# Attention's last product in a hybrid encoder block: values against turned probabilities, with the value tile rearranged

## The chip, the core and the metric

The kernel runs on one core of a Trainium2 chip. The metric is device time in microseconds (us), median of three runs. The engines are TensorE (PE), VectorE (DVE), ScalarE (ACT), GpSimd (POOL) and SyncE (SP), which only issues transfers here. Each has its own queue and works it off in order; they meet at semaphores.

## What is computed

One layer over 512 tokens of width 1024, in float32. Of the three branches between the two norms, the change touches attention: 8 heads of 64 columns, causal, with a forget bias.

```python
def forgetting_attention(q, k, v, f_logit, b_f):
    log_f = jax.nn.log_sigmoid((f_logit + b_f).astype(jnp.float32))
    F = jnp.cumsum(log_f, axis=1)
    ...
        logits = jnp.einsum('bqhd,bkhd->bhqk', q_i, k).astype(jnp.float32) * scale
        decay = F_q_i.transpose(0, 2, 1)[..., :, None] - F_k[..., None, :]
        mask = k_pos[None, :] <= pos_i[:, None]
        logits = jnp.where(mask, logits + decay, NEG_INF)
        p = jax.nn.softmax(logits, axis=-1)
        return jnp.einsum('bhqk,bkhd->bqhd', p.astype(v.dtype), v)
...
x = x + mixed @ w_out[l]
h = rms_norm(x, ffn_norm[l])
a, b = jnp.split(h @ w_gate_up[l], 2, axis=-1)
x = x + (jax.nn.silu(a) * b) @ w_down[l]
```

## The kernel before

**Numbers in two parts.** TensorE is fed tiles of type float32r. So that nothing of float32 is lost, each operand is kept as a high part (a copy in float32r) and a low part (the value less its high part). A product of two such operands takes three passes: high by high, high by low, low by high. For a weight tile of 128x1024, ACT writes the high part (`split_hi`, L741) and DVE the low one (`split_lo`, L1009). For an operand ACT runs `operand_hi` (L744) and DVE `operand_lo` (L1016).

**Units.** Weights come in units of 256 KB through three slots (`raw`, `whi`, `wlo`). `whole` (L450) is the product of a unit with all eight blocks of the activations: 24 matmuls of 512 columns, lines 436, 438 and 440.

**Stages.** norm, front, pair (four times, two heads each), mix (four times), out, the feed-forward stages. All loops are written out by hand on each engine, and the order of the work is the order of the code.

**A pair on TensorE** (L521 to L590): q and k (`whole` on units 0 and 1), five of eight blocks of v (unit 2), the logits of head 0 (L539, L541), two more blocks of v, the logits of head 1, the last block; conv's value column (unit 3), the turn of v by transposes (L549, bank 7), conv's gate (unit 4); the turn of head 0's probabilities (`turn_probs`, L561), six blocks of unit 5, the turn of head 1's, the last two blocks. Then comes what is changed: for each head, four blocks of tokens, three matmuls each (L584, L586, L588), of 512, 384, 256 and 256 columns. The stationary tile is the turned v of both heads, high (`V_HI`) or low (`V_LO`), 128 tokens by 128 value columns; the moving tile is a head's turned probabilities, high or low (`PT`). Head 0 goes to bank 7, head 1 to bank 3; half of the 128 rows of each result belong to the other head's columns, and are not used.

**What follows on ACT and DVE.** ACT writes the high part of a head's 64 rows from its bank (L862), DVE the low part (L1222), which frees the bank. DVE then runs the short convolution (L1230 to L1237, into `CY`), ACT and DVE split `CY`, then unit 8 of the stage's own count, that is unit 2 of the next pair. The next pair's q and k are worked out of banks 0 and 1 (ACT L820, L826, L831; DVE L1154, L1162). TensorE waits ahead of the next logits for banks 0 and 1 to be free and for `op_hi` (L528 to L530), which stands for L1154, L1162 and L831.

In mix, TensorE runs two gates (`whole`, twice) before `project` (L607) reads the attention output.

Of the kernel before, what the change touches and what calls it, by code (L numbers as in the profile page):

```python
# [19 lines left out]
ALU = mybir.AluOpType  # L20
# [38 lines left out]
    "op_hi": dict(norm=8, front=8, pair=15, mix=2, out=8, ffn_first=1, ffn=3),  # L59
    "op_lo": dict(front=4, pair=1, mix=2, ffn_first=1, ffn=3),  # L60

    "scalar_tile": dict(norm=12, front=2, out=8, ffn_first=3, ffn=3, down_a_end=4,
                        down_b_end=16),
    "vector_tile": dict(norm=8, front=2, pair=1, mix=2, ffn_first=3, ffn=3, down_b_end=16),
    "row_max": dict(pair=2), "exp_done": dict(pair=2), "probs": dict(pair=2),

    "vector_step": dict(norm=19, front=23, pair=15, mix=2, ffn_first=6, ffn=3, down_b_end=9),
# [12 lines left out]
def count(what, stage, i, k):  # L80

    before = 0
    for s, times, _ in STAGES:
        if s == stage:
            return before + i * RAISED[what].get(s, 0) + k
        before += times * RAISED[what].get(s, 0)
# [15 lines left out]
def hybrid_block(nc, x, attn_norm, w_in, b_forget, b_gate, w_proj_attn, pool_w, pool_scale,  # L102
# [26 lines left out]
    with ExitStack() as ctx:  # L129
# [3 lines left out]
        def sem(name):  # L133
            return ctx.enter_context(nc.semaphore(name))
# [30 lines left out]
        QS, KK = [T0, T0 + S], [T0 + 2 * S, T0 + 3 * S]  # L165
        K_LO, V_HI, V_LO = [T0 + S * j for j in (4, 5, 6)]

# [20 lines left out]
        def op(at, n=S, rows=slice(0, P)):  # L188
            return operands[rows, at:at + n]

        def half_rows(a):

            return slice(a * HD, (a + 1) * HD)

        def pt_at(j):

            return PT_AT[j] + (P if j == TB - 1 else 0)
# [7 lines left out]

        VT, CV, CB, CY = 0, 1, 2, 3
        GA, ACC, TMP = 0, 3, 4
# [41 lines left out]
        scalar_tile, vector_tile = sem("scalar_tile"), sem("vector_tile")  # L249
        row_max, exp_done, probs = sem("row_max"), sem("exp_done"), sem("probs")  # L250
        vector_step = sem("vector_step")
        consts = sem("consts")
# [11 lines left out]
        def wait_free(eng, b, stage, i, k):  # L264

            eng.wait_ge(free[b], count(f"free{b}", stage, i, k))
# [154 lines left out]
        def _(pe):  # L421
# [99 lines left out]
            with pe.Fori(0, WB) as i:  # L521
# [52 lines left out]
                for a, b, k in ((0, 7, 2), (1, 3, 5)):  # L574
                    wait_free(pe, 7, "pair", i, 1)
                    for j in range(TB):
                        wait_free(pe, 3 + j, "pair", i, 3 + a)
                    begin(b, "pair", i, k)
                    for j in range(TB):
                        first = min(j, TB - 2)  # L580
                        dst = banks[b][:, first * P:S]
                        n, at = S - first * P, PT_AT[j]
                        vj = slice(j * P, (j + 1) * P)
                        nc.tensor.matmul(dst, op(V_HI)[:, vj], op(PT[a][0] + at, n),  # L584
                                         start=(j == 0), stop=False)
                        nc.tensor.matmul(dst, op(V_HI)[:, vj], op(PT[a][1] + at, n),  # L586
                                         start=False, stop=False)
                        mm = nc.tensor.matmul(dst, op(V_LO)[:, vj], op(PT[a][0] + at, n),  # L588
                                              start=False, stop=(j == TB - 1))
                    mm.then_inc(full[b], 1)  # L590


            with pe.Fori(0, DB // 2) as i:
# [10 lines left out]
                whole(1, "mix", i, 1, 1, H_HI, H_LO)  # L604
                wait_free(pe, 7, "pair", 3, 2)
                wait_free(pe, 3, "pair", 3, 5)
                project(2, [(0, 3, 1), (1, 4, 1)])  # L607
                whole(2, "mix", i, 3, 1, H_HI, H_LO)
                pe.wait_ge(op_lo, count("op_lo", "pair", 3, 1))
                project(4, [(2, 5, 1), (2, 6, 1)])  # L610
# [123 lines left out]
        def _(act):  # L734
# [8 lines left out]
            def operand_hi(dst, src, scale=1.0):  # L743
                nc.scalar.activation(dst, src, ACT.Copy, scale=scale).then_inc(op_hi, 1)  # L744
# [71 lines left out]
            with act.Fori(0, WB) as i:  # L816
# [32 lines left out]
                wait_full(act, 7, "pair", i, 1)  # L849
                operand_hi(op(V_HI), banks[7][:])  # L850
                split_hi("pair", i, 6)
# [7 lines left out]
                for a, b, k in ((0, 7, 2), (1, 3, 5)):  # L859
                    rows = slice(a * HD, (a + 1) * HD)  # L860
                    wait_full(act, b, "pair", i, k)
                    operand_hi(operands[rows, bass.ds(BR[0][0] + i * S, S)], banks[b][rows, :])  # L862
                act.wait_ge(vector_tile, count("vector_tile", "pair", i, 1))
# [123 lines left out]
        def _(dve):  # L987
# [161 lines left out]
            with dve.Fori(0, WB) as i:  # L1149
# [54 lines left out]
                split_lo("pair", i, 5)  # L1204
                operand_lo("pair", i, 4, op(V_HI), op(V_LO), banks[7][:], None, 7)
                split_lo("pair", i, 6)
# [12 lines left out]
                wait_free(dve, 2, "pair", i, 2)  # L1219
                for a, b in ((0, 7), (1, 3)):  # L1220
                    rows = slice(a * HD, (a + 1) * HD)
                    operand_lo("pair", i, 13 + a, operands[rows, bass.ds(BR[0][0] + i * S, S)],  # L1222
                               operands[rows, bass.ds(BR[0][1] + i * S, S)], banks[b][rows, :],
                               None, b)

# [203 lines left out]
```

## Time and profile before

| | |
|---|---|
| Time, median of 3 runs | 845.84 us (845.74 to 847.63) |
| Span of the profiled execution | 846.0 us |
| TensorE busy | 828.2 us, 98% |
| TensorE weight loads (beside the matmuls) | 679.0 us, 80% |
| DVE busy | 433.0 us, 51% |
| ACT busy | 294.4 us, 35% |
| DMA, share of 16 engines | 32% |
| One pair | 45.0 us, four of them from about 58 to 235 us |

The span runs from the first to the last instruction of the one execution that was profiled, and lies 0.16 us above the median of the runs, so a difference in the span is read as one in the time. Busy time of matmuls overlaps: a matmul of 512 columns is shown as 0.39 us long, while the next starts 0.23 us after it.

### The profile page before, as it was taken

To read this page: it belongs to the slowest core of one execution; us is meant where nothing else is said; L and a number is where in the kernel's file an instruction comes from. 1 tells how busy PE (TensorE), PEld (TensorE's weight loads), DVE (VectorE), ACT (ScalarE), POOL (GpSimd) and SP (SyncE) were. 2 spreads that over 40 slices of the span, in tenths; PEclk is the share of its full clock that TensorE was granted. 3 is DMA by queue.
4 is the path that set the end of the run, shared out by engine and by line. 5 is a ranking of instruction groups with operands and counts; after the bars stand their busy time and mean duration, and the time that the engine had idled before them with its cause. 6 is when DMAs were issued, how large, how long until landed. Compare 5 with 4: busy or idle time off the path is not lost.

```text
span 846.0 us, 11118 instructions
## 1 busy us (share of the span) xinstructions
PE 828.2 (98%) x3691; PEld 679.0 (80%) x3691; DVE 433.0 (51%) x636; ACT 294.4 (35%) x466; POOL 3.6 (0%) x12
## 2 busy tenths in 40 slices
PE   5999999999999999999999999999999999999996
PEld 5777878787888888888888888888888888888884
DVE  6867585767753444344344555555555555323224
ACT  7355354443533222223323533222222222213113
POOL 1000000000000000000000000000000000000000
PEclk9989999999999999999999999999999999999998
DMA  6321222222223323333533223333333342222212
GB/s 212 100 76 50 76 74 74 74 74 75 74 75 100 99 76 98 101 97 99 173 125 100 76 75 99 99 99 99 99 99 99 99 119 101 102 97 89 94 46 100
DMA packets 126857, 80.27 MB, mean 95 GB/s; under 512 B 4796, under 2 KB 116980, under 8 KB 126836
## 3 DMA queue, kind: packets, MB, share of 16 engines
q1 hardware_dynamic: 126836, 80.00, 32.0%
q8 instruction: 12, 0.20, 0.1%
q14 instruction: 9, 0.07, 0.0%
HBM read 77.89 MB, written 2.10 MB: 95 GB/s over the span
## 4 chain that ended last, share of the span: by engine, by line
PE 95%; DVE 3%; ACT 1%; DMA 0%; issue 0%; SPq 0%; DVEq 0%; ACTq 0%
PE bank L436 23%; PE bank L440 23%; PE bank L438 23%; PE bank L628 6%; PE bank L626 6%; PE bank L630 6%; PE bank L541 1%; PE bank L539 1%; PE bank L561 1%; PE bank L467 1%; DVE operands L1018 1%; PE bank L586 1%; PE bank L584 1%; PE bank L588 1%; ACT work L747 0%; DMA big_x<-in_x_dram 0%
## 5 line engine op out<-in xcount | busy, mean ns | idle before, releaser
L436 PE MATMUL bank<-operands,whi 128*128 128x512 f32 x872 | 342.4, 393 | 0.9 <-DVE operands L1018 0.9
L438 PE MATMUL bank<-operands,whi 128*128 128x512 f32 x872 | 339.6, 390 | 0.0
L440 PE MATMUL bank<-operands,wlo 128*128 128x512 f32 x872 | 339.6, 389 | 0.0
L1009 DVE TENSOR_TENSOR wlo<-raw,whi 128x1024 fp32r<-128x1024 f32 x139 | 170.1, 1225 | 216.6 <-ACT whi L741 214.5
L436 PEld LDWEIGHTS bank<-operands,whi 128*128 128x128 f32 x872 | 163.9, 188 | 37.0 <-issue 3.3
L440 PEld LDWEIGHTS bank<-operands,wlo 128*128 128x128 f32 x872 | 163.8, 188 | 34.2
L438 PEld LDWEIGHTS bank<-operands,whi 128*128 128x128 f32 x872 | 163.9, 188 | 33.7 <-issue 0.2
L741 ACT CAST whi<-raw 128x1024 fp32r<-128x1024 f32 x139 | 145.0, 1043 | 130.1 <-PE bank L630 97.9
L626 PE MATMUL bank<-whi,operands 128*128 128x512 f32 x240 | 93.4, 389 | 0.0
L630 PE MATMUL bank<-whi,operands 128*128 128x512 f32 x240 | 93.4, 389 | 0.0
L628 PE MATMUL bank<-wlo,operands 128*128 128x512 f32 x240 | 93.4, 389 | 0.0
L744 ACT ACTIVATE operands<-work 128x512 f32 (+1 forms) x38 | 24.0, 632 | 166.1 <-DVE work L1337 112.9
L626 PEld LDWEIGHTS bank<-whi,operands 128*128 128x128 f32 x240 | 45.1, 188 | 9.4
L630 PEld LDWEIGHTS bank<-whi,operands 128*128 128x128 f32 x240 | 45.1, 188 | 9.4
L628 PEld LDWEIGHTS bank<-wlo,operands 128*128 128x128 f32 x240 | 45.1, 188 | 9.2
L1016 DVE TENSOR_TENSOR operands<-work,operands 128x512 f32 (+1 forms) x38 | 26.3, 692 | 36.0 <-ACT operands L744 36.0
L878 ACT ACTIVATE work<-bank,vecs 128x512 f32<-128x512 f32 x24 | 16.6, 690 | 79.2 <-PE bank L440 79.2
L1250 DVE TENSOR_TENSOR work<-bank,work 128x512 f32<-128x512 f32 x24 | 15.8, 688 | 41.2 <-PE bank L440 29.6
L1329 DVE TENSOR_TENSOR work<-bank,big_y 128x512 f32<-128x512 f32 x22 | 15.2, 691 | 36.7 <-PE bank L440 36.7
L747 ACT ACTIVATE work<-work 128x512 f32<-128x512 f32 (+1 forms) x24 | 15.2, 632 | 50.8 <-DVE work L1326 49.5
L1016 DVE TENSOR_TENSOR operands<-bank,operands 128x512 fp32r<-128x512 f32 (+4 forms) x44 | 21.7, 539 | 20.3 <-ACT operands L744 20.3
L840 ACT ACTIVATE big_y<-big_y,stat 128x128 f32<-128x128 f32 (+3 forms) x32 | 17.6, 552 | 31.0 <-DVE stat L1191 31.0
(124 smaller groups left out, 444.2 us busy)
## 6 DMA issues: line engine op xcount, KB each, us to landing
raw<-in_w_in_dram SPq DMA_DIRECT2D x106, 256.0 KB, 3.1
raw<-in_w_gate_up_dram SPq DMA_DIRECT2D x88, 256.0 KB, 3.1
raw<-in_w_down_dram SPq DMA_DIRECT2D x44, 256.0 KB, 3.0
raw<-in_w_out_dram SPq DMA_DIRECT2D x16, 256.0 KB, 3.1
big_x<-in_x_dram SPq DMA_DIRECT2D x4, 512.0 KB, 3.7
raw<-in_w_proj_attn_dram SPq DMA_DIRECT2D x8, 256.0 KB, 2.8
raw<-in_w_proj_pool_dram SPq DMA_DIRECT2D x8, 256.0 KB, 3.2
raw<-in_w_proj_conv_dram SPq DMA_DIRECT2D x8, 256.0 KB, 2.9
```

The source lines that it names most:

```text
L436: nc.tensor.matmul(banks[b][:, 0:width], whi[:, s, w], op(hi + k * S), start=a, stop=False)
L438: nc.tensor.matmul(banks[b][:, 0:width], whi[:, s, w], op(lo + k * S), start=False, stop=False)
L440: mm = nc.tensor.matmul(banks[b][:, 0:width], wlo[:, s, w], op(hi + k * S), start=False, stop=z)
L626: nc.tensor.matmul(banks[b][:], op(hi + at, P), whi[:, s, w], start=a, stop=False)
L628: nc.tensor.matmul(banks[b][:], op(hi + at, P), wlo[:, s, w], start=False, stop=False)
L630: mm = nc.tensor.matmul(banks[b][:], op(lo + at, P), whi[:, s, w], start=False, stop=z)
L741: nc.scalar.copy(whi[:, s, :], raw[:, s, :]).then_inc(w_hi, 1)
L744: nc.scalar.activation(dst, src, ACT.Copy, scale=scale).then_inc(op_hi, 1)
L840: e = nc.scalar.activation(lg, lg, ACT.Exp, bias=stat[:, 16 + at:17 + at], accum_out=stat[:, 24 + at:25 + at])
L878: nc.scalar.activation(wk(GA + br), banks[b][:], ACT.Sigmoid, bias=vecs[:, bass.ds(i * 2 + (V_GATE + br * DB + mm), 1)]).then_inc(free[b], 1)
L1009: nc.vector.tensor_tensor(wlo[:, s, :], raw[:, s, :], whi[:, s, :].bitcast(F32), ALU.subtract).then_inc(w_lo, 1)
L1016: ins = nc.vector.tensor_tensor(lo, src, hi.bitcast(F32), ALU.subtract)
```

## The change

The v tile is kept once for each head, `VV[a]`. For each block of 128 tokens it has 128 columns: 64 of the head's v in high part, and the same 64 in low part beside them. Head 0 has its high part in the left half, head 1 in the right. So the stationary tile has high and low at once, and two passes (against the high and the low part of the probabilities) leave two halves in the bank: rows of high v, and rows of low v. Their sum is the head's output (with the product of both low parts, which three passes left out).

On TensorE the third matmul of each block is gone. ACT writes the high part of v in two instructions (64 of every 128 columns each), DVE the low part in two. After the products ACT copies the half with low v to SBUF (`PV_LO`), DVE adds the other half from the bank and stores the sum in `PV`, which frees the bank; ACT and DVE take high and low part from `PV`. The low parts now count on `op_lo`, three a pair, and TensorE in mix waits for that count where it waited for banks 7 and 3.

```diff
@@ -57,12 +57,13 @@
     "op_hi": dict(norm=8, front=8, pair=15, mix=2, out=8, ffn_first=1, ffn=3),
-    "op_lo": dict(front=4, pair=1, mix=2, ffn_first=1, ffn=3),
+    "op_lo": dict(front=4, pair=3, mix=2, ffn_first=1, ffn=3),
     "scalar_tile": dict(norm=12, front=2, out=8, ffn_first=3, ffn=3, down_a_end=4,
                         down_b_end=16),
     "vector_tile": dict(norm=8, front=2, pair=1, mix=2, ffn_first=3, ffn=3, down_b_end=16),
     "row_max": dict(pair=2), "exp_done": dict(pair=2), "probs": dict(pair=2),
+    "v_lo_part": dict(pair=2),
     "vector_step": dict(norm=19, front=23, pair=15, mix=2, ffn_first=6, ffn=3, down_b_end=9),
 }
@@ -163,7 +164,11 @@
         QS, KK = [T0, T0 + S], [T0 + 2 * S, T0 + 3 * S]
-        K_LO, V_HI, V_LO = [T0 + S * j for j in (4, 5, 6)]
+        K_LO = T0 + 4 * S
+        VV = [T0 + 5 * S, T0 + 6 * S]
         PT_AT = [0, 4 * P, 7 * P, 9 * P]
@@ -192,6 +197,15 @@
             return slice(a * HD, (a + 1) * HD)
+        def v_part(a, low):
+            at = HD * (a if not low else 1 - a)
+            return op(VV[a]).rearrange("p (j c) -> p j c", c=P)[:, :, at:at + HD]
+        def v_turned(a):
+            return banks[7][:].rearrange("p (j c) -> p j c", c=P)[:, :, a * HD:(a + 1) * HD]
         def pt_at(j):
             return PT_AT[j] + (P if j == TB - 1 else 0)
@@ -203,7 +217,7 @@
         def wk(slot, n=S, rows=slice(0, P)):
             return work[rows, slot * S:slot * S + n]
-        VT, CV, CB, CY = 0, 1, 2, 3
+        VT, CV, CB, CY, PV_LO, PV = 0, 1, 2, 3, 4, 5
         GA, ACC, TMP = 0, 3, 4
         A1, SG, B1, HD_ = 0, 1, 2, 3
         JUNK_OUT, JUNK, FG = 5, 2, 4
@@ -248,6 +262,7 @@
         op_hi, op_lo = sem("op_hi"), sem("op_lo")
         scalar_tile, vector_tile = sem("scalar_tile"), sem("vector_tile")
         row_max, exp_done, probs = sem("row_max"), sem("exp_done"), sem("probs")
+        v_lo_part = sem("v_lo_part")
         vector_step = sem("vector_step")
         consts = sem("consts")
         pool_w_hi, pool_w_lo = sem("pool_w_hi"), sem("pool_w_lo")
@@ -581,11 +596,9 @@
                         dst = banks[b][:, first * P:S]
                         n, at = S - first * P, PT_AT[j]
                         vj = slice(j * P, (j + 1) * P)
-                        nc.tensor.matmul(dst, op(V_HI)[:, vj], op(PT[a][0] + at, n),
+                        nc.tensor.matmul(dst, op(VV[a])[:, vj], op(PT[a][0] + at, n),
                                          start=(j == 0), stop=False)
-                        nc.tensor.matmul(dst, op(V_HI)[:, vj], op(PT[a][1] + at, n),
-                                         start=False, stop=False)
-                        mm = nc.tensor.matmul(dst, op(V_LO)[:, vj], op(PT[a][0] + at, n),
+                        mm = nc.tensor.matmul(dst, op(VV[a])[:, vj], op(PT[a][1] + at, n),
                                               start=False, stop=(j == TB - 1))
                     mm.then_inc(full[b], 1)
@@ -602,11 +615,10 @@
                 whole(0, "mix", i, 0, 1, H_HI, H_LO)
                 whole(1, "mix", i, 1, 1, H_HI, H_LO)
-                wait_free(pe, 7, "pair", 3, 2)
-                wait_free(pe, 3, "pair", 3, 5)
+                pe.wait_ge(op_lo, count("op_lo", "pair", 3, 2))
                 project(2, [(0, 3, 1), (1, 4, 1)])
                 whole(2, "mix", i, 3, 1, H_HI, H_LO)
-                pe.wait_ge(op_lo, count("op_lo", "pair", 3, 1))
+                pe.wait_ge(op_lo, count("op_lo", "pair", 3, 3))
                 project(4, [(2, 5, 1), (2, 6, 1)])
                 whole(0, "mix", i, 5, 2, H_HI, H_LO)
                 whole(1, "mix", i, 6, 2, H_HI, H_LO)
@@ -847,7 +859,8 @@
                 wait_unit(act, "pair", i, 3)
                 nc.scalar.copy(wk(CV), banks[0][:]).then_inc(free[0], 1)
                 wait_full(act, 7, "pair", i, 1)
-                operand_hi(op(V_HI), banks[7][:])
+                nc.scalar.activation(v_part(0, False), v_turned(0), ACT.Copy)
+                operand_hi(v_part(1, False), v_turned(1))
                 split_hi("pair", i, 6)
                 wait_unit(act, "pair", i, 4)
                 nc.scalar.copy(wk(CB), banks[1][:]).then_inc(free[1], 1)
@@ -857,9 +870,13 @@
                         wait_full(act, 3 + j, "pair", i, 3 + a)
                         operand_hi(op(PT[a][0] + pt_at(j), S - j * P), banks[3 + j][:, j * P:S])
                 for a, b, k in ((0, 7, 2), (1, 3, 5)):
-                    rows = slice(a * HD, (a + 1) * HD)
                     wait_full(act, b, "pair", i, k)
-                    operand_hi(operands[rows, bass.ds(BR[0][0] + i * S, S)], banks[b][rows, :])
+                    nc.scalar.copy(wk(PV_LO, S, half_rows(a)), banks[b][half_rows(1 - a), :]
+                                   ).then_inc(v_lo_part, 1)
+                for a, b, k in ((0, 7, 2), (1, 3, 5)):
+                    rows = half_rows(a)
+                    wait_free(act, b, "pair", i, k)
+                    operand_hi(operands[rows, bass.ds(BR[0][0] + i * S, S)], wk(PV, S, rows))
                 act.wait_ge(vector_tile, count("vector_tile", "pair", i, 1))
                 operand_hi(opd(BR[2][0], i), wk(CY))
                 split_hi("pair", i, 8)
@@ -1202,7 +1219,11 @@
                                                       None, ALU.mult)
                     ins.then_inc(probs, 1)
                 split_lo("pair", i, 5)
-                operand_lo("pair", i, 4, op(V_HI), op(V_LO), banks[7][:], None, 7)
+                dve.wait_ge(op_hi, count("op_hi", "pair", i, 4))
+                for a in range(2):
+                    ins = nc.vector.tensor_tensor(v_part(a, True), v_turned(a),
+                                                  v_part(a, False).bitcast(F32), ALU.subtract)
+                ins.then_inc(free[7], 1)
                 split_lo("pair", i, 6)
                 split_lo("pair", i, 7)
                 for a in range(2):
@@ -1217,11 +1238,16 @@
                 nc.vector.tensor_tensor(wk(CV), banks[2][:], wk(CV), ALU.mult
                                         ).then_inc(free[2], 1)
                 wait_free(dve, 2, "pair", i, 2)
-                for a, b in ((0, 7), (1, 3)):
-                    rows = slice(a * HD, (a + 1) * HD)
+                for a, b, k in ((0, 7, 2), (1, 3, 5)):
+                    rows = half_rows(a)
+                    dve.wait_ge(v_lo_part, count("v_lo_part", "pair", i, a + 1))
+                    nc.vector.tensor_tensor(wk(PV, S, rows), banks[b][rows, :], wk(PV_LO, S, rows),
+                                            ALU.add).then_inc(free[b], 1)
+                for a, b, k in ((0, 7, 2), (1, 3, 5)):
+                    rows = half_rows(a)
+                    wait_free(dve, b, "pair", i, k)
                     operand_lo("pair", i, 13 + a, operands[rows, bass.ds(BR[0][0] + i * S, S)],
-                               operands[rows, bass.ds(BR[0][1] + i * S, S)], banks[b][rows, :],
-                               None, b)
+                               operands[rows, bass.ds(BR[0][1] + i * S, S)], wk(PV, S, rows))
                 def tap(k):
                     return vecs[:, bass.ds(i + (V_CONV + k * WB), 1)]
```

TensorE, head 0's product in a pair. Names: `operands` holds both v and the probabilities, and the bank is the output. Before:

```order
L584 MATMUL bank7<-operands 128x512 [waits free5,free6,free4,free7,free3]
L586 MATMUL bank7<-operands 128x512
L588 MATMUL bank7<-operands 128x512
L584 MATMUL bank7<-operands 128x384
L586 MATMUL bank7<-operands 128x384
L588 MATMUL bank7<-operands 128x384
```

And with the change:

```order
L599 MATMUL bank7<-operands 128x512 [waits free5,free6,free4,free7,free3]
L601 MATMUL bank7<-operands 128x512
L599 MATMUL bank7<-operands 128x384
L601 MATMUL bank7<-operands 128x384
L599 MATMUL bank7<-operands 128x256
```

One matmul of three is gone from each block, 8 in a pair and 32 in all; the waits ahead of the first are the same.

ACT, from the products of a pair to the high part of `CY` (`work`, the last row). Before:

```order
L744 ISA [waits full7]
L744 ACTIVATE operands<-bank7 64x512
L258 REGISTER_ALU
L744 ISA [waits full3]
L744 ACTIVATE operands<-bank3 64x512
L863 REGISTER_ALU
L744 ISA [waits vector_tile]
L744 ACTIVATE operands<-work 128x512
```

And with the change:

```order
L874 COPY work<-bank7 64x512 [waits full7]
L273 REGISTER_ALU
L874 COPY work<-bank3 64x512 [waits full3]
L756 ISA [waits free7]
L756 ACTIVATE operands<-work 64x512
L756 ISA [waits free3]
L756 ACTIVATE operands<-work 64x512
L880 REGISTER_ALU
L756 ISA [waits vector_tile]
L756 ACTIVATE operands<-work 128x512
```

Two copies stand ahead, and both high parts now come behind them and each behind a wait for DVE's sum.

DVE, from the convolution's first product (`bank2`) to its next step. Before:

```order
L1217 TENSOR_TENSOR work<-bank2,work 128x512 [waits free0]
L266 REGISTER_ALU
L1014 REGISTER_ALU [waits free2]
L1016 ISA [waits op_hi]
L1016 REGISTER_ALU
L1016 TENSOR_TENSOR operands<-bank7,operands 64x512
```

And with the change:

```order
L1238 TENSOR_TENSOR work<-bank2,work 128x512 [waits free0]
L281 REGISTER_ALU
L1244 TENSOR_TENSOR work<-bank7,work 64x512 [waits v_lo_part,free2]
L1244 TENSOR_TENSOR work<-bank3,work 64x512 [waits v_lo_part]
L1031 REGISTER_ALU [waits free7]
L1033 ISA [waits op_hi]
L1033 REGISTER_ALU
L1033 TENSOR_TENSOR operands<-work,operands 64x512
```

Two additions stand ahead of the low parts, each waiting for a copy of ACT.

## Rows read from the trace of the kernel before

**Rows 1.** The page: span, and busy time of each engine.

```profile
span 846.0 us, 11118 instructions
...
PE 828.2 (98%) x3691; PEld 679.0 (80%) x3691; DVE 433.0 (51%) x636; ACT 294.4 (35%) x466; POOL 3.6 (0%) x12
```

**Rows 2.** Waits of PE: waiter <- releaser, total us, times, longest; first and last.

```profile
PE bank L460 <- DMA bias_f<-in_b_forget_dram: 6.1, 1, 6.1
...
PE bank L485 <- DVE operands L1016: 0.8, 1, 0.8
```

**Rows 3.** Stretches: us, busy us (instructions) of each engine, granted clock, DMA share, GB/s.

```profile
60.00:105.00 45.00, 45.00 (x210) 35.90 (x209) 29.59 (x55) 19.53 (x42) 0.00 (x0) 1.00 0.26 69
...
195.00:240.00 45.00, 45.00 (x209) 35.91 (x208) 31.50 (x57) 20.76 (x44) 0.00 (x0) 1.00 0.25 70
```

**Rows 4.** Groups by line: busy us, mean ns of one, idle before; one of three alike.

```profile
L588 PE MATMUL bank<-operands 128*128 128x256 f32 (+2 forms) x32 | 10.3, 323 | 0.0
```

**Rows 5.** Timeline of PE, second pair: start, us, engine, line, operation.

```profile
140.90 0.39 PE L584 MATMUL bank<-operands 128*128 128x512 f32 x1
141.13 0.39 PE L586 MATMUL bank<-operands 128*128 128x512 f32 x1
...
142.82 0.40 PE L584 MATMUL bank<-operands 128*128 128x512 f32 x1
...
144.75 0.39 PE L436 MATMUL bank<-operands,whi 128*128 128x512 f32 x1
```

**Rows 6.** Timeline of DVE, same pair; in brackets the idle time before and its releaser.

```profile
139.70 1.69 DVE L1016 TENSOR_TENSOR operands<-bank,operands 128x512 fp32r<-128x512 f32 x4 [1.91 <-ACT operands L744]
...
143.99 0.68 DVE L1016 TENSOR_TENSOR operands<-bank,operands 64x512 f32 x1 [2.01 <-ACT operands L744]
145.83 0.69 DVE L1016 TENSOR_TENSOR operands<-bank,operands 64x512 f32 x1 [1.15 <-ACT operands L744]
...
151.29 1.23 DVE L1009 TENSOR_TENSOR wlo<-raw,whi 128x1024 fp32r<-128x1024 f32 x1
...
157.09 1.39 DVE L1162 TENSOR_TENSOR operands<-bank,operands 64x512 fp32r<-64x512 f32 x2 [1.90 <-ACT operands L826]
```

**Rows 7.** Timeline of ACT, same stretch.

```profile
143.14 0.59 ACT L744 ACTIVATE operands<-bank 64x512 f32 x1 [2.65 <-PE bank L588]
145.05 0.59 ACT L744 ACTIVATE operands<-bank 64x512 f32 x1 [1.32 <-PE bank L588]
149.69 0.63 ACT L744 ACTIVATE operands<-work 128x512 f32 x1 [4.04 <-DVE work L1237]
...
155.86 1.20 ACT L826 ACTIVATE operands<-bank 64x512 fp32r<-64x512 f32 x2 [2.30 <-PE bank L440]
157.09 1.25 ACT L831 CAST operands<-operands 64x512 fp32r<-64x512 f32 x2
```

**Rows 8.** Timeline of PE: the third pair's first matmul of logits.

```profile
159.06 0.28 PE L539 MATMUL bank<-operands 128*128 128x256 f32 x1
```

**Rows 9.** Groups by line and shape, 60 to 240 us: busy us, mean ns, idle before.

```profile
L1016 DVE TENSOR_TENSOR operands<-bank,operands 128x256 fp32r<-128x256 f32 x8 | 3.3, 416 | 0.0
...
L744 ACT ACTIVATE operands<-bank 128x256 fp32r<-128x256 f32 x8 | 3.1, 393 | 0.0
```

**Rows 10.** Timeline of ACT behind the high part of v, second pair.

```profile
133.40 0.59 ACT L853 COPY work<-bank 128x512 f32<-128x512 f32 x1 [3.21 <-PE bank L440]
```

**Rows 11.** Timeline of DVE behind the low part of v, second pair.

```profile
134.97 1.23 DVE L1009 TENSOR_TENSOR wlo<-raw,whi 128x1024 fp32r<-128x1024 f32 x1 [2.29 <-ACT whi L741]
```

**Rows 12.** Stretches in front (columns as in rows 3).

```profile
46.00:48.00 2.00, 2.00 (x11) 1.56 (x11) 1.87 (x2) 1.32 (x3) 0.00 (x0) 1.00 0.81 234
...
50.00:52.00 2.00, 2.00 (x5) 1.14 (x5) 1.76 (x2) 0.00 (x0) 0.00 (x0) 0.50 0.00 0
...
54.00:56.00 2.00, 2.00 (x8) 1.58 (x7) 0.72 (x1) 2.00 (x5) 0.00 (x0) 0.71 0.57 163
```

## The prediction

> **What bounds the kernel now.** I read the page's line of busy times first: TensorE is busy for 828.2 of 846.0 us, DVE and ACT for half and a third [rows 1]. Then the waits of TensorE: four entries, from 6.1 us down to 0.8, all of them at the start or in front [rows 2]. None lies in the pairs, where the change is: there TensorE is busy for all of every stretch of 45.00 us, at a granted clock of 1.00 (2.4 GHz), and DMA has a share of a quarter [rows 3]. So time that TensorE is spared in a pair is time of the kernel, as long as nothing new makes it wait, and a transfer, an ACT or a DVE instruction costs nothing as long as it is done when TensorE comes to need it. The rest is two questions: how much TensorE is spared, and whether the longer way from the products to the low parts stays under cover.
>
> **What TensorE is spared.** The group of L588 shows 32 matmuls and 10.3 us busy, and the groups of L584 and L586 the same [rows 4]. That is not the gain: matmuls overlap (the row at 140.90 is 0.39 us long, the next starts at 141.13), so it is starts that count. Head 0's twelve matmuls run from 140.90 to 142.82, which is 1.92 us; head 1's from there to the next block's first matmul at 144.75, 1.93 us [rows 5]. In each block the three passes have the same number of columns and the third goes, so a third of 3.85 us goes: 1.28 us a pair, and four times that is **5.13 us**. The bounds on this term: nothing if the places stay empty (a rival, below), and 10.3 us by the busy time, which would need matmuls that don't overlap; I take the starts, since they are what the same matmuls do in the same place. The moving columns, the number of weight loads for a matmul and the waits ahead of the first one are unchanged.
>
> The Trainium skill ("TensorE: Matmul & The Clock Gate", Back-to-back issue gap) gives a matmul N columns divided by 2.4 GHz plus 2.5 ns. For 512, 384, 256 and 256 columns that is 216, 163, 109 and 109 ns, 0.60 us a head, and an estimate by that page is 4.8 us for eight heads. The rows show 0.23 us where it has 0.216, and they decide.
>
> **What is added to the split of v.** ACT writes the high part in two instructions of 256 elements, at 0.39 us each by the nearest row, instead of one of 512 at 0.59; DVE the low part in two at 0.42 [rows 9] instead of one of 0.69. The new ones have runs of 64 columns, which no row has; dearest they would cost what one of 512 does, 0.6 and 0.7 us each. Some 0.15 us more on each engine, at worst 0.7. Behind it ACT next idles for 3.21 us until TensorE is done [rows 10], DVE for 2.29 us [rows 11], and the products start only at 140.90, some 9 us later. Nothing comes through: 0.
>
> **Head 1 comes sooner.** Its products wait for the low parts of its probabilities, which DVE ends at 139.70 + 1.69 = 141.39 [rows 6]. Head 1 now starts at 142.82 - 0.64 = 142.18 instead of 142.82 [rows 5]. So 0.79 us of slack are left of 1.43: 0. That DVE work idles for 1.91 us ahead [rows 6] and hangs on TensorE's transposes alone, so the split of v can't push it.
>
> **The new way from the products to the low parts.** I replay the second pair. Before, ACT starts on head 0 at 143.14, 0.32 us after the end of its products, and on head 1 at 145.05, 0.30 us after [rows 5, 7]. Ends are now 142.18 and 144.75 - 1.28 = 143.47, so ACT starts the copies at 142.50 and 143.77; each takes 0.59 us (an ACT instruction of 64x512 from a bank, [rows 7]; both bounds of it are near, a copy or cast of this size from anywhere shows 0.59 to 0.63). From ACT's end to DVE's start rows show 0.26 us (143.73 to 143.99) and 0.19 (145.64 to 145.83) [rows 6, 7]; I take 0.26. DVE adds at 143.35 to 144.04 and, behind the second copy (144.36), at 144.62 to 145.31, by 0.69 us a piece: a DVE instruction with a bank and SBUF as inputs on 64 rows [rows 6]. ACT writes the high parts from SBUF at about 144.4 to 145.0, and, 0.13 us behind the second sum, at 145.44 to 146.07, by 0.63 us [rows 7]. DVE writes the low parts at 145.35 to 146.04 and at 146.33 to **147.02**. Before, the last low part ended at 145.83 + 0.69 = 146.52 [rows 6]. So DVE's tail (the convolution, `CY`, unit 8, the low parts of q and k) is **0.5 us later** by the clock on the wall, while TensorE is 1.28 us earlier: together 1.8 us of slack are used in each step from pair to pair.
>
> What stood behind, and still fits: unit 8's low part ends at 151.29 + 1.23 = 152.52 [rows 6], now 153.02. TensorE needs it 48 matmuls behind the products. From 144.75 to 159.06 it has 63 matmuls [rows 5, 8], 0.227 us each, so 48 are 10.90 us and the need is at 155.65, now 154.37: 1.35 us are left. Then k. ACT's L826 starts at 155.86 when TensorE is done with k, after an idle 2.30 us [rows 7]; it now would start at 154.58 with 0.5 us of idle left. DVE's L1162 starts at 157.09 after an idle 1.90 us [rows 6], now at 155.81 with 1.90 - 0.50 - 1.28 = 0.12 us left. It ends 1.39 us later at 158.48 (ACT's L831 at 158.34), and the logits begin at 159.06 [rows 6 to 8]: 0.58 us. So 0.12 + 0.58 = **0.70 us** of cover remain ahead of the logits, three times in the kernel. Behind the fourth pair stand two gates, 48 matmuls again, before the attention output is read at about 10.9 us; the low parts are there 3.5 us behind the products' end, and the gates don't need them. Sum of all waits: 0.
>
> **Sum.** 845.84 - 5.13 = **840.7 us**, and a span of about 840.9.
>
> **Rivals.**
>
> *TensorE waits at the logits (part of the gain).* DVE's tail is the only place with little cover. Were each of the four hand-overs between ACT and DVE 0.26 us longer than I put it (twice the dearest on a row), the tail would be 1.04 us later, 0.34 beyond the cover; three steps give 1.0 us, and the time is 841.7. At 0.9 us beyond the cover in each step it is 843.4, which is about no gain. For it: the order of waits crosses between the engines twice now where it crossed once. Against: all pieces have near rows.
>
> *Nothing is gained.* The same wait at 1.3 to 1.7 us beyond the cover (a tail 2 us or more longer than the replay) would put the pairs at ACT's and DVE's pace, and only the fourth keeps its 1.28 us: 844.6 us, within the bound. That asks for added instructions at twice the rows' durations. That the compiler keeps the third matmul is excluded by the order of instructions: 8 fewer in a pair.
>
> *The clock falls (slower).* In front, TensorE is busy throughout, yet the granted clock goes from 1.00 (11 matmuls in 2 us) to 0.50 (5 in 2 us, 1.2 GHz), and is back in the stretch from 54 to 56 us [rows 12]. What runs ahead of the fall are 16 matmuls with 8 rows. A fall as long as that one, from about 48.5 to 55 us, costs about half of 6.5 us, 3.2 us. A pair has thin matmuls too, with 64 rows (L541), and a third of the full ones at its end now goes. Were that to bring one such fall into every pair, the time would be 840.7 + 12.8 = 853.5; from two falls in all, it is slower than before. Against it: the clock is 1.00 in all four pairs [rows 3], and 16 full matmuls and 48 more still follow there with no gap. The Trainium skill (same page, Part 1) has the throttle released by how busy the engine has been; by that rule there is no fall here, as no idle time is added, but the rows show a fall with the engine busy for the whole stretch, so the rule alone does not exclude it.
>
> **How the numbers follow.** Forecast, no wait: 0.82. Part of the gain: 0.07. Nothing gained: 0.05. Clock: 0.03. Another loss that I don't see: 0.03. A measurement of this kernel can tell about 0.3%, 2.5 us, from no change, so the bound is 843.3. Faster: 0.82 and most of the 0.07, 0.88. Same: the rest of it and the nothing, 0.07. Slower: 0.05. The range goes from 839.5 (the term 1.2 us larger, a quarter, or a faster median) up to 843.3: the median of before may stand up to 1.8 us under a single run, and the partial case is taken in.
>
> **What would show it.** TensorE's instructions fall by 32 in 3691, its busy time by up to 10.3 us, but the span by 5.1. The products take 2.57 us a pair (16 starts) and a pair 43.7 instead of 45.0. The list of TensorE's waits has no new entry; an entry at L539's place behind the low part of k, or an issue wait there, is the first rival. DVE's idle time ahead of the low part of k shrinks from 1.90 to about 0.1 us, ACT's ahead of k from 2.30 to 0.5. The first addition starts about 1.2 us behind head 0's last matmul start. The granted clock stays 1.00 from 60 us on. I am wrong if the pair's period falls by less than 1.2 us, if head 1's products start later than 1.3 us behind head 0's, or if a later stage gives the 5 us back.

## The result, and the profile after

| | before | after |
|---|---|---|
| First measurement, median | 845.79 us (845.65 to 847.63, 4 runs) | 839.74 us (839.62 to 840.14, 4 runs) |
| Ratio, first measurement | | 0.9923, 95% interval 0.9910 to 0.9935 |
| Ratio, more runs of the same two kernels | | 0.9942, 95% interval 0.9927 to 0.9957 |
| Span of the profiled execution | 846.0 us | 838.0 us |
| One pair, logits to logits | 45.02 us | 43.75 us |

The change makes the kernel faster. The forecast was 840.7 us, a ratio of 0.9939. The first measurement gave more: by its ratio the time is 845.84 * 0.9923 = 839.3 us, just below the low end of 839.5 (its median, 839.74 us, lies 0.2 us above that end). The second, with 23 runs of before and 6 of after, gave 0.9942.

The page of after, against [rows 1]:

```profile
span 838.0 us, 11082 instructions
...
PE 820.6 (98%) x3659; PEld 672.4 (80%) x3659; DVE 438.7 (52%) x648; ACT 299.2 (36%) x478; POOL 3.6 (0%) x12
```

TensorE has 32 matmuls fewer, DVE and ACT 12 instructions more each and 5.7 and 4.8 us more work. TensorE's waits answer to [rows 2]: four entries again (first and last shown), at the start and in front, none in the pairs, and the granted clock is 1.00 in all four pairs.

```profile
PE bank L475 <- DMA bias_f<-in_b_forget_dram: 6.5, 1, 6.5
...
PE bank L500 <- DVE operands L1033: 0.8, 1, 0.8
```

TensorE's timeline of the second pair's products, against [rows 5], and the third pair's logits, against [rows 8] (start, us, engine, line, operation):

```profile
137.28 0.39 PE L599 MATMUL bank<-operands 128*128 128x512 f32 x1
...
138.56 0.40 PE L599 MATMUL bank<-operands 128*128 128x512 f32 x1
...
154.16 0.28 PE L554 MATMUL bank<-operands 128*128 128x256 f32 x1
```

A head takes 1.28 us instead of 1.92. ACT and DVE behind it, against [rows 6] and [rows 7] (in brackets the idle time before, and what ended it):

```profile
138.76 0.58 ACT L874 COPY work<-bank 64x512 f32<-64x512 f32 x1 [1.89 <-PE bank L601]
140.06 0.58 ACT L874 COPY work<-bank 64x512 f32<-64x512 f32 x1 [0.71 <-PE bank L601]
...
141.49 0.63 ACT L756 ACTIVATE operands<-work 64x512 f32 x1 [0.20 <-DVE work L1244]
...
150.96 1.20 ACT L838 ACTIVATE operands<-bank 64x512 fp32r<-64x512 f32 x2 [1.05 <-PE bank L455]
```

```profile
139.44 0.68 DVE L1244 TENSOR_TENSOR work<-bank,work 64x512 f32<-64x512 f32 x1 [1.09 <-ACT work L874]
140.67 0.69 DVE L1244 TENSOR_TENSOR work<-bank,work 64x512 f32<-64x512 f32 x1 [0.54 <-ACT work L874]
141.55 1.44 DVE L1033 TENSOR_TENSOR operands<-work,operands 64x512 f32 x2 [0.19 <-issue]
...
152.19 1.39 DVE L1179 TENSOR_TENSOR operands<-bank,operands 64x512 fp32r<-64x512 f32 x2 [0.51 <-ACT operands L838]
```

The order is the one of the replay. The low parts end at 142.99, 5.71 us behind the products' start, where before they ended 5.62 behind it (146.52 - 140.90): the longer way delays them by 0.1 us, not 0.5.

But 8.0 us of span is more than four pairs give, which is 4 * 1.27 = 5.1 us. The first pair's logits start at 69.01 before and at 66.66 after: **2.35 us of the 8.0 lie ahead of all that was changed.** This the experiments had to explain.

### The profile page after: what moved, and what is told of

The parts are those of the page before. It is cut to its first block, busy times and chain, and to the rows that moved or that the text cites. A ratio compares the mean times of both kernels' runs of the same rounds, so it can differ in the third digit from the quotient of the medians.

```text
span 838.0 us, 11082 instructions
## 1 busy us (share of the span) xinstructions
PE 820.6 (98%) x3659; PEld 672.4 (80%) x3659; DVE 438.7 (52%) x648; ACT 299.2 (36%) x478; POOL 3.6 (0%) x12
## 4 chain that ended last, share of the span: by engine, by line
PE 94%; DVE 3%; ACT 1%; DMA 1%; SPq 1%; issue 0%; DVEq 0%; ACTq 0%
PE bank L451 23%; PE bank L455 23%; PE bank L453 23%; PE bank L642 6%; PE bank L640 6%; PE bank L638 6%; PE bank L556 1%; PE bank L554 1%; PE bank L576 1%; DMA raw<-in_w_in_dram 1%; DVE operands L1035 1%; PE bank L601 1%; PE bank L599 1%; ACT work L759 1%; PE bank L652 0%
## 5 line engine op out<-in xcount | busy, mean ns | idle before, releaser
L756 ACT ACTIVATE operands<-work 128x512 f32 (+2 forms) x46 | 29.1, 632 | 166.9 <-DVE work L1363 112.9
L1033 DVE TENSOR_TENSOR operands<-work,operands 128x512 f32 (+2 forms) x46 | 31.8, 692 | 37.1 <-ACT operands L756 36.0
L1355 DVE TENSOR_TENSOR work<-bank,big_y 128x512 f32<-128x512 f32 x22 | 15.2, 691 | 36.7 <-PE bank L455 36.7
L1352 DVE TENSOR_TENSOR work<-bank,big_y 128x512 f32<-128x512 f32 x22 | 15.2, 691 | 12.3 <-PE bank L455 7.3
```

The costliest lines, as they stand in the source:

```text
L1033: ins = nc.vector.tensor_tensor(lo, src, hi.bitcast(F32), ALU.subtract)
```

## The experiments

**Both kernels again, five rounds.** No edit.

> The kernel before, word for word, timed against itself. Its trace on record spans 846.0 us; the one of the changed kernel spans 838.0, of which four pairs explain 5.1 us, and 2.35 us lie ahead of the first pair's logits, in code that the change does not touch. Theory A (the front differs from execution to execution, by where the granted clock falls, and the change has nothing to do with it): this run's logits of the first pair start anywhere from 66.7 to 69 us, and the ratio is 1.000 within 0.001. Theory B (the front is a property of the program): the logits start again at 69.0 us, and the clock is again 0.50 from about 48.5 to 55 us.

> The changed kernel, word for word, in more rounds. Prediction on record: 840.7 us, a ratio of 0.9939 (5.13 us). First measurement: 839.74 us, 6.05 us less than before. Theory A expects 5.1 us and a spread of the front around it, so 0.993 to 0.995. Theory B expects 6.0 us again, 0.9928, and the logits of the first pair at 66.7 us.

The kernel before against itself: 0.9996 (0.9984 to 1.0008). Its profiled execution took 845.50 us and spans 843.7, not 846.0, and the logits start at 66.76, not at 69.01. The changed kernel: 0.9942 (0.9927 to 0.9957), logits at 67.25. So the same program has two fronts, and theory A holds: the front differs from execution to execution. The stretches from 50 to 54 us show how (us, busy us and instructions of PE, PEld, DVE, ACT, POOL, then the granted clock, DMA share, GB/s); the kernel before in the new execution, against [rows 12]:

```profile
50.00:52.00 2.00, 2.00 (x6) 1.58 (x5) 1.72 (x2) 1.43 (x3) 0.00 (x0) 0.50 0.00 0
52.00:54.00 2.00, 2.00 (x7) 1.59 (x6) 0.05 (x1) 2.00 (x4) 0.00 (x0) 0.66 0.83 221
54.00:56.00 2.00, 2.00 (x10) 1.62 (x9) 1.82 (x2) 0.74 (x2) 0.00 (x0) 1.00 0.19 54
```

The clock falls later and is back earlier. In the trace on record 15 matmuls in a row run at half clock, with 0.42 us or more to the next start (from 48.45 us on), and from the first full unit (15.85) to the logits it is 53.16 us. In the new one it is 7 matmuls, from 50 us on, and 51.64 us; the changed kernel has 7 too, and 51.67 us (14.99 to 66.66). (Two expectations further on say 16 and 10; the timelines show 15 and 7.) The long fall began while the 16 matmuls with 8 rows still ran (nine of them had started by 48.1 us, the last starts at 51.01), the short one behind all of them (the last starts at 49.05 us). The other 0.7 us between the two executions lie ahead of the first full unit, 15.85 against 15.12 us. The times show two groups, too: of 23 runs of before, 11 lie between 845.2 and 846.2 us, 12 between 847.4 and 848.8, none between. Of the 10 runs of after, 6 lie between 839.6 and 840.6, 4 between 841.3 and 842.1. The mean granted clock of each run goes with them: 0.992 or 0.993 in all 12 upper runs of before, 0.994 or 0.995 in all 11 lower ones; of after, 0.994 in three of the four upper ones (the fourth, 841.39 us, has 0.996) and 0.996 or 0.997 in the lower ones. The first measurement had all four of after in its lower group, and one of before's four in the upper one.

**Each half of the change alone, five rounds.** First, the way of before without the pass over the low part of v (that term is left out of the result):

```diff
-                        nc.tensor.matmul(dst, op(V_HI)[:, vj], op(PT[a][1] + at, n),
-                                         start=False, stop=False)
-                        mm = nc.tensor.matmul(dst, op(V_LO)[:, vj], op(PT[a][0] + at, n),
+                        mm = nc.tensor.matmul(dst, op(V_HI)[:, vj], op(PT[a][1] + at, n),
                                               start=False, stop=(j == TB - 1))
```

> The kernel before without the third pass (low part of v against the high part of the probabilities, which is left out of the result); all of ACT and DVE stays as before. It does the first half of the change alone. If the starts on TensorE are all that counts, it takes what the change takes: 5.13 us less than before, 840.7 us, and the same 43.75 us for a pair. If the longer way on ACT and DVE costs something, this one is faster than the changed kernel by it. If the change owes some of its 6.0 us to something beside the third pass, this one is slower than it, by up to 0.9 us.

Then the new way with a third matmul put back (the result then counts the high part of the probabilities twice):

```diff
-                        mm = nc.tensor.matmul(dst, op(VV[a])[:, vj], op(PT[a][1] + at, n),
+                        nc.tensor.matmul(dst, op(VV[a])[:, vj], op(PT[a][1] + at, n),
+                                         start=False, stop=False)
+                        mm = nc.tensor.matmul(dst, op(VV[a])[:, vj], op(PT[a][0] + at, n),
                                               start=False, stop=(j == TB - 1))
```

> The changed kernel with a third matmul in each block again (the high part of the probabilities a second time, which the result then counts twice): 96 matmuls as before, and the new way on ACT and DVE. Theory (starts on TensorE alone): 845.8 us, no change against before, and a pair of 45.02 us. If the new way costs time by itself it is slower than before; by the replay it uses 0.5 us of a cover of 1.98, so it should not. If the program's shape moves the front, it shows here as up to 0.9 us less than before.

The old way with two passes: 0.9940 (0.9921 to 0.9958), beside 0.9942 for the whole change, and a pair of 43.75 us (logits at 112.86, 156.61 and 200.37). The new way with three: 0.9991 (0.9980 to 1.0002), and a pair of 45.03 us (112.96, 157.99). The pass is worth all of the gain, and the longer way on ACT and DVE is free in the pairs. The second interval allows from 0.2 us of loss to 1.7 us of gain by the new way; what there is lies behind the last matmul, see below.

**How much cover the tail has, three rounds.** In the changed kernel, DVE runs the convolution's first step three and five times:

```diff
-                step(nc.vector.tensor_scalar(wk(CY), wk(CV), tap(2), None, ALU.mult))
+                for _ in range(3):
+                    step(nc.vector.tensor_scalar(wk(CY), wk(CV), tap(2), None, ALU.mult))
```

> The changed kernel with the convolution's first step on DVE (0.49 us, a start every 0.64 us) run three times in a row instead of once, the result unchanged: DVE's tail between the attention output and the next pair's k is 1.28 us longer. The changed kernel's trace shows 0.51 us of idle on DVE ahead of the low part of k, and 0.58 us from its end to the logits, a cover of 1.09 us; the prediction had put it at 0.70. Theory A (that cover is all there is, and the rest becomes a wait of TensorE at the logits, three times): 0.2 us a step, 0.6 us in all, a pair of 43.95 us. By the cover as predicted: 0.58 us a step, 1.7 us in all. Theory B (the way on ACT and DVE is covered by more than that, since TensorE can start the first logits while the last are awaited): no change, a pair of 43.75 us.

> The same with the step run five times: the tail is 2.56 us longer. Theory A: 2.56 - 1.09 = 1.47 us of wait at the logits of the second, third and fourth pair, 4.4 us in all, so all but 0.7 us of the change's gain is gone and a pair takes 45.2 us. By the cover as predicted: 1.86 a step, 5.6 us in all, slower than before. Theory B: no change.

My price of a step was off: five of them take 2.57 us where one takes 0.49, so a repeat is 0.52 us, and the tail is 1.04 and 2.08 us longer, not 1.28 and 2.56. With two repeats the ratio to before is 0.9938 (0.9920 to 0.9956), which can't be told from the changed kernel's, but the pairs show it: the logits start at 67.35, 111.42, 155.63 and 199.79, so a pair takes 44.07, 44.21 and 44.16 us, 0.32 to 0.46 more than 43.75. With four repeats the first two steps are 45.11 and 45.22 us, 1.36 and 1.47 more. Both doses give the same cover: 1.04 - 0.40 = 0.64 and 2.08 - 1.42 = 0.66 us. Theory A, a limited cover, holds in kind, and B is out; the cover is neither 1.09 nor 0.70. Idle time in a trace is not all cover: with two repeats DVE's low part of k ends at 109.69 + 1.39 = 111.08, and the logits it holds up start at 111.42, which is 0.34 us of the hand-over; and the first of them takes 0.31 us to the next, not 0.21. 1.09 - 0.34 - 0.10 is 0.65.

```profile
109.69 1.39 DVE L1179 TENSOR_TENSOR operands<-bank,operands 64x512 fp32r<-64x512 f32 x2
```

```profile
111.42 0.38 PE L554 MATMUL bank<-operands 128*128 128x256 f32 x1 [0.17 <-issue]
111.73 0.38 PE L556 MATMUL bank<-operands 64*128 64x256 f32 x1
```

With four repeats TensorE waits at a second place too, for unit 8's low part, four times for 0.3 us:

```profile
153.51 0.49 PE L451 MATMUL bank<-operands,whi 128*128 128x512 f32 x1 [0.29 <-DVE wlo L1026]
```

In the changed kernel that low part ends at 149.00 us and is needed at 150.76, 1.76 us later, as the replay has it once the way is 0.4 us shorter than forecast; 2.08 us use that up. It adds nothing to the pair: DVE works without a gap from unit 8's low part to k's (152.15 to 157.48 us), and the logits wait for DVE's end in any case.

The third step with four repeats took 46.70 us, 1.5 more than the other two, and the ratio of that kernel is 1.0026 (1.0011 to 1.0040), its ten runs from 846.7 to 851.6 us. Its stretches at the third pair's logits (columns as above) show why:

```profile
160.00:162.00 2.00, 2.00 (x5) 1.21 (x5) 1.48 (x3) 0.00 (x0) 0.00 (x0) 0.61 0.79 199
162.00:164.00 2.00, 2.00 (x7) 1.27 (x5) 1.86 (x5) 0.00 (x0) 0.00 (x0) 0.53 0.21 63
164.00:166.00 2.00, 2.00 (x7) 1.00 (x7) 1.82 (x5) 1.11 (x5) 0.00 (x0) 1.00 0.00 0
```

```profile
112.59 0.38 PE L554 MATMUL bank<-operands 128*128 128x256 f32 x1 [0.62 <-DVE operands L1179]
...
157.81 0.38 PE L554 MATMUL bank<-operands 128*128 128x256 f32 x1 [0.60 <-DVE operands L1179]
...
204.51 0.38 PE L554 MATMUL bank<-operands 128*128 128x256 f32 x1 [0.60 <-DVE operands L1179]
```

Behind the second of these waits and eight matmuls of logits, four of them with 64 rows, the granted clock fell to the level of 1.2 GHz. Behind the other two, as long and in the same place, it stayed at 1.00 (112 to 118 and 204 to 210 us). The mean granted clock of all ten runs of this kernel is 0.987 to 0.993, below the changed kernel's 0.994 to 0.997, and it falls as the time grows. So the fall that the prediction had as its slower rival does occur in a pair once TensorE waits there, but what picks the pair is not shown. The changed kernel, where nothing waits, has none in either of its traces.

**The fall in front, five rounds.** If the matmuls with 8 rows bring the fall, padding them should take it away. In both kernels, with rows of zeros:

```diff
-            nc.gpsimd.memset(op(SEL, H * P, slice(0, H)).bitcast(F32), 0.0).then_inc(consts, 1)
+            nc.gpsimd.memset(op(SEL, H * P).bitcast(F32), 0.0).then_inc(consts, 1)
...
-            sel = op(SEL, H * P, slice(0, H)).rearrange("p (h c) -> p h c", h=H)
+            sel = op(SEL, H * P).rearrange("p (h c) -> p h c", h=H)
...
+            nc.gpsimd.memset(op(F_HI, 2 * S).bitcast(F32), 0.0).then_inc(consts, 1)
...
-                    sel = op(SEL + h * P, P, slice(0, H))
-                    nc.tensor.matmul(banks[b][:], sel, op(F_HI, S, slice(0, H)),
+                    sel = op(SEL + h * P, P)
+                    nc.tensor.matmul(banks[b][:], sel, op(F_HI, S),
...
-                    nc.tensor.matmul(banks[b][:], sel, op(F_LO, S, slice(0, H)),
+                    nc.tensor.matmul(banks[b][:], sel, op(F_LO, S),
...
+            dve.wait_ge(consts, 9)
```

> The changed kernel, with the spread of the forget sums in front done by matmuls of 128 rows instead of 8: the selecting tile and the sums are padded with rows of zeros (two memsets of GpSimd), the result is the same. In all six traces so far the granted clock falls from 1.00 to 0.50 behind the 16 matmuls with 8 rows, for 10 matmuls of 0.43 us in some executions and for 16 in others, and the times of each kernel lie in two clusters 2 us apart. Theory A (the few rows bring the fall): the clock stays at 1.00 after 40 us, the two clusters become one, and the time falls by 2.0 to 3.3 us, to about 837 to 838 us. Theory B (the fall has another cause, or zeros count like missing rows): the same two clusters at 839.7 to 842 us.

> The same padding in the kernel before. Theory A: one cluster at about 843 us, and against it the changed kernel with the same padding gains 5.1 us (0.9939), with a narrower interval than the unpadded pair, since the only part of the time that differed from execution to execution is gone. Theory B: two clusters at 845.5 and 847.7 us as before.

Beside the rows, the edit gives GpSimd a memset more and DVE a wait for it at the start. The changed kernel, padded: 837.82 us (837.74 to 838.71, 4 runs), 0.9894 (0.9877 to 0.9911). The kernel before, padded: 843.20 us (842.85 to 844.02, 5 runs), 0.9961 (0.9946 to 0.9976). The clock stays up, in the padded changed kernel:

```profile
48.00:50.00 2.00, 2.00 (x12) 1.70 (x12) 1.41 (x5) 1.26 (x3) 0.00 (x0) 1.00 0.00 0
50.00:52.00 2.00, 2.00 (x10) 1.48 (x10) 1.83 (x3) 0.96 (x3) 0.00 (x0) 1.00 0.00 0
52.00:54.00 2.00, 2.00 (x10) 1.64 (x9) 0.66 (x1) 2.00 (x5) 0.00 (x0) 1.00 0.29 53
```

The way from the first full unit to the logits is 49.95 us (16.07 to 66.02; before, padded, 49.92), against 51.67 with the short fall and 53.2 with the long one. Theory A holds: the fall costs 1.7 or 3.2 us. The 1.5 us between the two are most of what parts the groups, which lie 2.1 us apart; the rest is not settled, and may be the start (the first full unit begins at 14.99 to 16.25 us in the traces with the short fall, at 15.85 and 15.91 in the two with the long one). The mean granted clock of all nine padded runs is 0.997 to 0.999, above every run of before. The 16 matmuls take as long (45.09 to 49.31 us in the padded kernel before, 45.17 to 49.36 in the other), and the rows added are zeros, so what takes the fall away is the rows. How many thin matmuls it needs was not measured. The padded changed kernel is the fastest of all; its interval lies below that of the changed kernel in the second measurement. Against the padded kernel before it gains 843.20 - 837.82 = 5.4 us (5.3 by the means), where the expectation had 5.1, and the stretch behind the last matmul, which the next paragraph is about, is alike in these two.

**What is left.** Two executions with the short fall, before at 845.50 and after at 839.77 us, differ by 5.7. The logits of the four pairs and the products behind them account for 5.11 (228.71 - 66.76 against 224.78 - 66.66 is 3.83, and the fourth pair's products give 1.28), the start for 0.1 (15.12 against 14.99), and the stretch behind the last matmul's start for 0.5: 843.7 - 835.23 = 8.47 against 838.0 - 830.02 = 7.98. There, before needs 4.0 us from the end of DVE's last instruction to the end of the span, and after 3.1; up to that instruction after is 0.35 us slower (4.85 against 4.50), which leaves 0.5. That is no effect of fewer matmuls: the old way with two passes has 8.5 us and 4.0, like before, the new way with three has 8.0 and 3.1, and the padded kernel before has 7.6 and 3.1. It goes with the program and not with what was changed in the pairs. Its cause was not looked for further, and stays open.

## Why the prediction was right, and where it was wrong

**What bounds the kernel: right.** TensorE has no wait in the pairs before or after, and what it is spared is what the kernel gains.

**The term of the third pass: right.** Forecast 1.28 us a pair and 5.13 in all, from the starts; the traces show 45.02 - 43.75 = 1.27 and 5.1. The busy time fell by 828.2 - 820.6 = 7.6 us, but 2.3 of them are the longer fall: the kernel before with the short fall is busy for 825.9 us, so like with like the difference is 5.3. The upper bound of 10.3 us, from busy times that overlap, was never near. The spacing in the Trainium skill ("TensorE: Matmul & The Clock Gate", Back-to-back issue gap: N divided by 2.4 GHz plus 2.5 ns) would have given 4.8, an estimate by that page; the rows decided rightly.

**The split of v: right.** ACT's two instructions take 0.38 and 0.37 us, DVE's two 0.75 together, with 64-column runs no dearer than one run of 256. ACT idles for 3.15 us a little later, as before (3.21), so nothing came through.

**The new way: right in order, its delay too large.** Forecast 0.5 us later, measured 0.1. The term that was mis-sized is the hand-over from ACT to DVE: I took 0.26 us, from rows where DVE's instruction has an address from a register and an ISA instruction holds the wait; the additions carry their wait themselves and start 0.10 us behind the copy (139.34 to 139.44) and 0.03 us (140.64 to 140.67). A further 0.1 us comes from TensorE to ACT: the copies, which carry their wait too, start 0.20 us behind head 0's products (138.56 to 138.76), where I had 0.32. That the place of the wait makes the difference is read from these rows, and no run tests it. DVE's idle time ahead of k's low part is 0.51 us, not 0.12.

**The cover: wrong in how it was counted.** I added idle time and the gap to the logits, and took the sum as cover. The doses show 0.65 us of 1.09: a wait that holds a matmul up costs a hand-over of 0.34 us and 0.1 us to the next start as well. Had the way taken the 0.5 us that I gave it, the cover would have been 0.26 and not 0.70 us, and my partial rival would have begun at little more than a third of the delay I named. The result did not hang on it.

**The rivals.** No part of the gain was lost to a wait. The fall of the clock did not come into the pairs, but the trace with four repeats shows that it can, behind one of three waits of 0.6 us. So that rival and the first hang together: a wait at the logits costs its own length and may bring 1.5 us of half clock besides, while the thin matmuls alone bring none in the pairs. The rival also read its row wrongly in one point: of the 16 matmuls with 8 rows, nine and not all had started when the clock fell in that trace. Its cost, 3.2 us, was right. The Trainium skill's rule ("TensorE: Matmul & The Clock Gate", Part 1) ties the throttle to how busy the engine has been; it would not tell the fall in front, with TensorE busy for all of each stretch, from the padded kernel, which is as busy and has none. The measurement decides.

**The range: wrong, and this is the step that failed.** "How the numbers follow" set the low end at 839.5, "the term 1.2 us larger, a quarter, or a faster median". The term was not larger; the spread of the measurement was mis-sized, and the time outside the pairs was put at nothing. Behind it stood a misreading in the first part: the span of 846.0 us was tied to the median of 845.84. A span lies about 1.8 us below its execution's time (838.0 and 839.77, 843.7 and 845.50), so the profiled execution of before was the one of 847.63 us, with the long fall, and the other two, by their times, had the short one. The three times on record already had the two groups in them, 2 us apart, and the trace had their cause, the fall in front, which I priced only as a rival of the change.

What the first measurement shows in its place, by the means of its four runs each (846.2 and 839.8 us), is 6.4 us: 5.1 from the pairs as forecast, 0.5 behind the last matmul, for which the forecast had nothing, and 0.5 because one of before's four runs lay in the upper group and none of after's; the rest, 0.3, is of the size of the differences at the start. The second draw, with 12 of 23 and 4 of 6 runs in the upper group, came out at 0.9942, so that it meets the forecast of 0.9939 this closely is in part luck, as the first miss was. With groups 2 us apart and few runs, the ratio of two equal kernels may come out up to 2 us off, so a forecast of 5.1 us needed a range from about 838.7 up (an estimate from the groups). The mechanism and its size stood; the spread around it was taken too narrow on the side of a larger gain.

## What to carry to other kernels

When TensorE bounds a kernel, price a removed matmul by the distance between starts in the same place, and replay the new way of the other engines against the waits that TensorE has there; cover is what is left after the hand-over and the slower first matmul, not the idle time in the trace. Where high and low part of a narrow operand fit side by side into one stationary tile, a third of the passes goes for two small copies and additions off the path. And before reading a difference of one per cent, look at the runs one by one and at the stretches where the granted clock falls: a part of the program that the change does not touch, here the fall in front, can cost 1.7 to 3.2 us beside a change worth 5.1.

## What the runs showed of the hardware

The granted clock fell to 1.2 GHz with TensorE busy for 100% of each stretch, during or behind 16 matmuls with 8 rows, for 7 or 15 matmuls, depending on the execution; with the same matmuls padded to 128 rows by zeros it did not fall, in either kernel, and the time fell by 0.39% (before) and to 0.9894 of before (changed kernel).

It also fell in a pair behind a wait of 0.60 us and matmuls of 64 rows. In the same trace it stayed at 1.00 behind two waits of 0.62 and 0.60 us with the same matmuls, and without a wait they ran at 1.00 in every trace.

An ACT copy of 64 rows that reads one half of the partitions and writes the other takes 0.58 us, as long as a straight one of that size (0.59).
